# Three buffers for expert weights up to the last slots, and the last slot's weights requested before the second last's

## What is computed

```
gp = softmax(x @ w_rg + b_rg); gsel = top_k(gp, 1)          # 4 groups
ep = softmax(el_sel);          topv, topi = top_k(ep, 2)    # 2 of 4 experts in the group
weights = gp_sel * topv / sum(topv)
g = einsum('nd,edf->nef', x, w_e_gate)                      # w_e_gate, w_e_up: 16 x 1024 x 256
u = einsum('nd,edf->nef', x, w_e_up)
act = silu(g) * u * combine[:, :, None]
out = einsum('nef,efd->nd', act, w_e_down)                  # w_e_down: 16 x 256 x 1024
x = x + gate2 * out;  y = rms_norm(x, norm_final_g)
```

## Time and profile before

| what | us |
|---|---|
| median of 3 runs | 733.85 |
| lowest and highest of them | 733.02, 736.99 |
| the profiled execution, its own time | 732.28 |
| its span, first to last instruction | 730.4 |
| TensorE busy in it | 695.0 (95%) |
| VectorE, ScalarE, GpSimd busy | 538.0, 346.3, 212.1 |
| mean granted clock of TensorE | 0.986 |

### The profile page before, as it was taken

The page is one execution under the profiler, slowest core; times in us unless marked ns, Lnnn a source line. Parts: engine busy times, 40 slices in busy tenths (PEclk is TensorE's granted clock), DMA queues, the critical chain, the costliest instruction groups (busy, mean ns, idle before and its releaser), DMA issues.

```text
span 730.4 us, 11140 instructions
## 1 busy us (share of the span) xinstructions
PE 695.0 (95%) x4420; PEld 606.8 (83%) x4420; DVE 538.0 (74%) x782; ACT 346.3 (47%) x455; POOL 212.1 (29%) x89
## 2 busy tenths in 40 slices
PE   5899999999999999999999999998879999998995
PEld 2599989999898899999999998886368888887863
DVE  3547999999678865946556663656789999987887
ACT  4552232533243443447365121134378888777634
POOL 3004222222200000000000000000129999899486
PEclk9999999999999999999999999999799999999999
DMA  9964154556616336612325326165948999989865
GB/s 324 377 187 132 58 174 174 175 182 211 229 29 128 33 107 123 118 61 67 107 65 170 111 73 220 68 259 197 420 152 334 392 409 401 421 328 376 336 236 203
DMA packets 75607, 149.10 MB, mean 204 GB/s; under 512 B 11302, under 2 KB 54626, under 8 KB 68836
## 3 DMA queue, kind: packets, MB, share of 16 engines
q1 hardware_dynamic: 61572, 125.28, 49.8%
q10 hardware_dynamic: 10096, 12.63, 4.8%
q0 software_dynamic: 3888, 10.49, 4.2%
HBM read 138.29 MB, written 20.05 MB: 217 GB/s over the span
## 4 chain that ended last, share of the span: by engine, by line
PE 79%; DMA 8%; DVE 6%; issue 3%; ACT 3%; POOL 1%; ACTq 1%; DVEq 0%; POOLq 0%; SPq 0%
PE psum L1009 36%; PE psum L1285 8%; PE psum L1327 7%; PE psum L944 4%; PE psum L514 4%; PE psum L515 4%; PE psum L520 4%; DMA down_raw<-in_w_e_down 2%; DMA xg<-h_d,slot_b 2%; PE psum L1231 2%; DMA w_raw<-in_w_ada 2%; PE psum L1161 1%; PE psum L1463 1%; DMA w_raw<-in_w_e_up 1%; PE psum L1028 1%
## 5 line engine op out<-in xcount | busy, mean ns | idle before, releaser
L1009 PE MATMUL psum<-hh,w_h 128*128 128x320 f32 x608 | 144.7, 319 | 0.2 <-issue 0.2
L1009 PE MATMUL psum<-hh,w_l 128*128 128x320 f32 x608 | 138.5, 309 | 0.0
L1009 PE MATMUL psum<-hl,w_h 128*128 128x320 f32 x608 | 138.4, 309 | 0.0
L1009 PEld LDWEIGHTS psum<-hh,w_h 128*128 128x128 f32 x608 | 99.8, 188 | 6.1 <-issue 4.0
L2070 DVE SCALAR_TENSOR_TENSOR psum<-conv,taps,psum 128x760 f32<-128x760 f32 x100 | 101.5, 1015 | 3.4
L1009 PEld LDWEIGHTS psum<-hl,w_h 128*128 128x128 f32 x608 | 101.6, 188 | 0.0
L1009 PEld LDWEIGHTS psum<-hh,w_l 128*128 128x128 f32 x608 | 101.6, 188 | 0.0
L692 POOL TENSOR_TENSOR ob<-obh,toff 128x260 bf16<-128x260 f32 x1 | 2.0, 1993 | 331.7 <-DVE obh L600 331.7
L726 POOL TENSOR_TENSOR down_l<-down_raw,down_h 128x2048 fp32r<-128x2048 f32 x16 | 87.6, 5477 | 21.2 <-ACT down_h L1838 20.9
L936 POOL TENSOR_TENSOR w_l<-w_raw,w_h 128x2048 fp32r<-128x2048 f32 x9 | 42.1, 4682 | 141.3 <-ACT w_h L1519 141.3
L2356 DVE TENSOR_TENSOR w_l<-w_raw,w_h 128x2048 fp32r<-128x2048 f32 x26 | 74.5, 2868 | 11.4 <-ACT w_h L1844 11.4
(11 more groups left out here) (384 smaller groups left out, 1395.8 us busy)
## 6 DMA issues: line engine op xcount, KB each, us to landing
w_raw<-in_w_in SPq DMA_DIRECT2D x20, 1024.0 KB, 7.0
down_raw<-in_w_e_down SPq DMA_DIRECT2D x17, 1024.0 KB, 12.5
w_raw<-in_w_ada SPq DMA_DIRECT2D x16, 1024.0 KB, 9.5
w_raw<-in_w_e_gate SPq DMA_DIRECT2D x13, 1024.0 KB, 7.2
w_raw<-in_w_e_up SPq DMA_DIRECT2D x13, 1024.0 KB, 11.0
w_more<-in_w_ada SPq DMA_DIRECT2D x8, 1024.0 KB, 10.1
y_d<-yy ACTq DMA_DIRECT2D x15, 512.0 KB, 8.1
y_d<-in_x_sample SPq DMA_DIRECT2D x12, 512.0 KB, 8.1
```

The source lines that it names most:

```text
L1009: mm = pe.matmul(psum[:, p + q, 0:HALF], w, r[:, k, q * HALF:(q + 1) * HALF], start=(k == 0 and x == 0), stop=(k == KT - 1 and x == 2))
```

## The change

Three buffers stay in use to the end: also inside the loops slot numbers map to buffers 1 and 2, and the very last slot gets buffer 0 (`final`), last used by slot 12. The down weights get a mapping of their own, `down_buffer`. All engines' loops now begin at slot 13 (`LOOP_AT`), GpSimd's gathers known up to slot 14. The waits inside SP's loop come from a table `wait_i` that `late_tables` fills with four more VectorE operations. At the end SP requests the last slot's gate and up weights before the second last's. The selection matrix `onehot0` moves, since its place now is in use by slot 15, and GpSimd waits for slot 15's down matmuls before the last two of `rows_back`. Early on, down weights 2 and 0 change places in the queue.

```
-POOL_LOOP_AT = 11
-SP_LOOP_AT = 15
-THREE_UNTIL = POOL_LOOP_AT
-FEWER = 2
...
+        held = r1[:, 19, 0:NS]
+        for n in range(2):
+            then(dve.tensor_scalar(held, iota[:, 0:NS], float(LOOP_AT + 2 - n), -2.0, ALU.is_ge, ADD))
+            then(dve.tensor_tensor(wait_i[:, n, :], held, iota[:, 0:NS], ADD))
...
-    def buffer(b, s):
-        return (0, 2, 1)[b % 3] if isinstance(b, int) and b < THREE_UNTIL else s
+    def buffer(b, s, final=False):
+        return (0, 2, 1)[b % 3] if isinstance(b, int) else 0 if final else 1 + s
+
+    def down_buffer(b, s, final=False):
+        return (1, 2, 0)[b % 3] if isinstance(b, int) else 0 if final else 1 + s
...
-        for b in range(POOL_LOOP_AT):
+        for b in range(LOOP_AT - 1):
             known_gather(b + 3)
             low(b % 2, b)
         pairs = pair_count(pool)
-        with pool.Fori(POOL_LOOP_AT // 2, pairs - 2) as p:
-            for b, s, _ in pair_slots(p):
-                counted_gather(1 - s, b + 3)
-                low(s, b)
-        counted_gather(0, 2 * pairs)
-        low(1, 2 * pairs - 3)
+        with pool.Fori(LOOP_AT // 2, pairs - 1) as p:
+            counted_gather(1, 2 * p + 3)
+            low(0, 2 * p)
+            counted_gather(0, 2 * p + 4)
+            low(1, 2 * p + 1)
...
         for t in range(NT):
+            if t == NT - 1:
+                pool.wait_ge(e_used, 2 * pairs)
+                carry(1, row_i[:, 0, 0:1])
             rows_back(t, 0, ysum[:, t, :])
...
-        down_weights(0, 0, own(0))
-        sp.wait_ge(h2_st, 16 * (NT + 1))
         down_weights(2, 0, own(2))
-        gate_up(3, 1, own(3))
-        for b in range(4, SP_LOOP_AT):
-            gate_up(b, b % 2, own(b))
-            down_weights(b - 1, 1 - b % 2, own(b - 1))
+        sp.wait_ge(h2_st, 16 * (NT + 1))
+        down_weights(0, 0, own(0))
+        gate_up(3, 1, own(3), 1)
+        for b in range(4, LOOP_AT):
+            gate_up(b, b % 2, own(b), b - 2)
+            down_weights(b - 1, 1 - b % 2, own(b - 1), b - 3)
         pairs = pair_count(sp)
-        with sp.Fori(SP_LOOP_AT // 2, pairs) as p:
+        with sp.Fori(LOOP_AT // 2, pairs - 1) as p:
             for b, s, _ in pair_slots(p):
-                gate_up(b, s, by_table(b))
-                down_weights(b - 1, 1 - s, by_table(b - 1))
-        down_weights(2 * pairs, 0, by_table(2 * pairs))
+                held = reuse(0, b), reuse(1, b - 1)
+                gate_up(b, s, by_table(b), held[0])
+                down_weights(b - 1, 1 - s, by_table(b - 1), held[1])
+        gate_up(2 * pairs, 0, by_table(2 * pairs), LOOP_AT, final=True)
+        down_weights(2 * pairs - 2, 0, by_table(2 * pairs - 2), 2 * pairs - 3)
+        gate_up(2 * pairs - 1, 1, by_table(2 * pairs - 1), 2 * pairs - 2)
+        down_weights(2 * pairs - 1, 1, by_table(2 * pairs - 1), 2 * pairs - 2)
+        down_weights(2 * pairs, 0, by_table(2 * pairs), final=True)
```

More of the change, by code:

```diff
@@ L724, in low @@
             pool.wait_ge(d_hi, b + 1)
-            n = buffer(b, s)
+            n = down_buffer(b, s)
             pool.tensor_tensor(down_l[n][:, :], down_raw[n][:, :], down_h[:, s, :].bitcast(F32), SUB).then_inc(d_lo, 1)
@@ L821, in _, with gate_up @@
                                  modrow[v:P:GRP, :]).then_inc(mod_st, 16)
-        def gate_up(b, s, pick):
-            n = buffer(b, s)
+        def gate_up(b, s, pick, used=None, final=False):
+            n = buffer(b, s, final)
+            if used is not None:
+                sp.wait_ge(gu_done, used)
             for c, name in enumerate(("w_e_gate", "w_e_up")):
@@ L830, in gate_up, with down_weights, reuse @@
                         chunk_used(sp, G0 - RING + 2 * n + c)
-                else:
-                    sp.wait_ge(gu_done, b - 2 if isinstance(b, int) and b <= THREE_UNTIL + 1 else b - 1)
                 dst, landed = (third_raw[:, c, :], more_in[c]) if n == 2 else (w_raw[:, 2 * n + c, :], raw_in[2 * n + c])
                 sp.dma_start(dst.rearrange("p (k n) -> p k n", k=KT), pick(a[name], "(p k) n -> p k n")).then_inc(landed, 16)
[L836 to L841, removed]
+        def down_weights(b, s, pick, used=None, final=False):
+            n = down_buffer(b, s, final)
+            if used is not None:
+                sp.wait_ge(e_used, used)
             sp.dma_start(down_raw[n][:, :].rearrange("p (k n) -> p k n", k=2),
                          pick(a["w_e_down"], "(p k) n -> p k n")).then_inc(down_in[n], 16)
+        def reuse(n, b):
+            return sp.value_load(wait_i[0:1, n, bass.ds(b, 1)], min_val=LOOP_AT - 3, max_val=NS)
         def own(b):
@@ L1402, in down @@
         def down(s, b, first=False, last=False):
-            wh, wl = down_h[:, s, :], down_l[buffer(b, s)][:, :]
+            wh, wl = down_h[:, s, :], down_l[down_buffer(b, s, last)][:, :]
             cols = lambda w, j, q: w[:, j * D + q * 512:j * D + (q + 1) * 512]
@@ L1425, in slot @@
                 turn_x(1 - s, u + s, b + 1)
-            wh, wl = w_h[:, 2 * s:2 * s + 2, :], low_of(b, s)
+            wh, wl = w_h[:, 2 * s:2 * s + 2, :], low_of(b, s, last)
             both = lambda w, k: w[:, :, k * DE:(k + 1) * DE]
@@ L1831, in _, with w_hi @@
                         act.dma_start(x2[:, t, :], src).then_inc(x2_in, 16)
-        def w_hi(s, b, u, c):
-            n = buffer(b, s)
-            landed = 16 * loads(b, s, u)
+        def w_hi(s, b, u, c, final=False):
+            n = (down_buffer if c == 2 else buffer)(b, s, final)
+            landed = 16 * (down_loads if c == 2 else loads)(b, s, u, final)
             if c == 2:
@@ L1843, in w_hi @@
                     act.wait_ge(raw_in[2 * n + c], landed + 16 * loads_of_slot(G0 + 2 * n + c) - 16)
[L1844 removed]
+                act.activation(w_h[:, 2 * s + c, :], raw_of(b, s, c, final), ACT.Copy).then_inc(e_hi, 1)
         for t in range(NT):
@@ L1914, in _, with slot @@
             x_high(0, 0, q, True)
-        def slot(b, s, u, last=False):
+        def slot(b, s, u, last=False, before_last=False):
             early = b if isinstance(b, int) else 2
@@ L1931, in slot @@
             act.activation(sil[:, :], psum[:, s, 0:DE], ACT.Silu).then_inc(sil_done, 1)
-            w_hi(s, b, u, 2)
+            w_hi(s, b, u, 2, last)
             if last:
@@ L1943, in _ @@
                 slot(*one)
-        slot(*pair_slots(pairs - 1)[0])
+        slot(*pair_slots(pairs - 1)[0], before_last=True)
         slot(*pair_slots(pairs - 1)[1], last=True)
```

31 lines of the change are left out of this document (17 added, 14 removed).

## The result

The changed kernel takes 739.43 us (median of 8 runs, 738.62 to 742.81); the kernel before, run beside it, 733.75. The ratio is 1.0089, 95% interval 1.0069 to 1.0109: slower, by 5.7 us in the medians and by 5 to 8 us by the interval. The profiled execution has its own time of 738.62, a span of 736.8 against 730.4 (+6.4), and a mean granted clock of 0.984 against 0.986.

The account below looks back on a forecast made before the run. It took the DMA engines to set the expert stage's pace by slot 9, 10.27 us a slot. 7.9 (late matmuls) + 1.6 (clock) - 0.2 (small parts) = +9.3 us, 743.2 us against the median; range 738.5 to 747.0.

Parts of the forecast that it names:

- rival B: DMA engines' mean share counts and ScalarE's later steps absorb part: slot 15 late by 2 to 5 us, 738; chance 0.10.
- The earlier requests for slots 13 and 14: Weights of slots 13 and 14 asked for one slot, 9.3 us, earlier; taken alone worth 0 to 1 us.
- The exchange of holes: TensorE's 2.12 us wait for slot 14's gather closes; 2.1 us come back waiting for slot 15's gather.
- The place in the queue: In SP's queue slot 15's gate/up weights pass behind three transfers: down 13, gate/up 16 and down 14.
- Landing of slot 15's up weights: Up to 685.2 us, less recovered DMA idle time of 0 to 3.2, taken as 1.5: 683.7.
- a sign of being wrong: Slot 15's up weights landing by 677, or weights over 0.5 us a slot faster than 10.3 from slot 11 on.
- Landing to matmuls: From slot 15's up weights landing to its matmuls 4.4 us: start at 688.1 instead of 680.19, 7.9 us later.
- The clock: After TensorE's idling before slot 15, eight matmuls at the lower clock cost 1.6 us, bounds 0 and 3.2.
- Small parts: VectorE table operations, register loads, GpSimd's wait hidden; slot 15's early down weights save at most 0.2: counted -0.2 us.
- A: The request order at the end costs nothing, only the earlier requests count: -2.9 us, 731.0; chance 0.05.
- C: The change's two halves cancel, within 3 us of 733.85, the expert stage's DMA never pausing; chance 0.06.
- D: SP's waits hold gate/up 16 until gate/up 15 is due: 733 to 734; no chance of its own, within 0.06.

Follow-up runs that it names:

- old-order version: The changed kernel with slot 15's gate and up weights again requested before slot 16's, three buffers kept; 731.67 us, ratio 0.9969 to the kernel before.
- one transfer less: The changed kernel with slot 14's down weights requested after slot 15's gate and up weights, not before them; 736.03 us, ratio 1.0043.
- one MiB more: The changed kernel with an extra 1 MiB HBM-to-HBM copy in SP's queue behind slot 7's down weights; 742.20 us, ratio 1.0131.
- the version with the fillers in slot 15: The changed kernel with 27 filler matmuls on TensorE before slot 15, where it stood idle; 738.63 us, ratio 1.0080.
- the old order with known gathers: The changed kernel with slot 15's weights requested before slot 16's and slot 15's gather a known one too; 733.26 us, ratio 0.9979.

## Why the prediction was right, and where it was off

The sign and the mechanism held: slot 15's weights late behind three transfers, a hole of TensorE, the clock's fall behind it. The size did not: 739.4 is 3.8 us under the forecast of 743.2, and 0.5 under the 739.9 that the forecast's own bounds gave. It lies in the stated range of 738.5 to 747.0 because that was drawn into rival B, which is luck as much as judgement, for B's condition (slot 15 late by 2 to 5 us) was not met: it was late by 7.3. By its own steps, on the profiled executions (+9.3 forecast, +6.4 measured):

- The earlier requests for slots 13 and 14: 0 to 1 us forecast. The old-order version carries them, and its ratio of 0.9969 is 2.3 us (0.4 to 4.1). The forecast was at the low end of that. The exchange of holes came as told: slot 14's 2.12 us are gone, slot 15's gather makes one of 0.92, less than the 2.1 forecast. But an execution of the kernel before has 0.23 and 0.90 in these places, so the change is not shown to have brought the exchange.
- The place in the queue: shown, by the old order (the loss is gone), one transfer less (less lost) and one MiB more (more lost).
- Landing of slot 15's up weights: 683.7 forecast, 682.5 measured. This is a mis-sized term. The idle time of the DMA engines, 3.2 us by the mean share, was taken to be recovered by 1.5, because the last engine of each transfer had seemed busy right through. The landing came 2.7 us before the 685.2 of nothing recovered, 2.5 counted from slot 12's gate issue. Part shows between the down weights of slots 12 and 13: 658.35 and 667.30, 8.95 us apart, against 10.26 in the same place before. From slot 11 to 13 they come 9.4 us apart, over 0.5 us faster than 10.3, which the prediction had named as a sign of being wrong. Windows over the whole stretch, from slot 12's gate issue to the landing that ends the three transfers, before and after:

```profile
626.77:685.16 58.39, 55.98 (x274) 46.76 (x273) 48.05 (x43) 44.50 (x47) 48.19 (x20) 1.00 0.95 373
626.62:682.51 55.89, 50.16 (x242) 41.26 (x240) 39.75 (x36) 36.48 (x39) 41.30 (x16) 1.00 0.97 391
```

The bytes are the same (21.8 and 21.9 MB). The engines' mean idle time went from 3.1 to 2.0 us (the shares of the queues add up to 94.6% and 96.5% of the stretch), which is 1.2 of the 2.5; the hole of 640 to 646 was filled, but the one that follows is longer than before (share 0.69 in 664 to 670, 1.9 us). The other 1.3 us are a higher rate at the same share: 419 GB/s in 646 to 664 at 1.01, where the kernel before had 391 in 646 to 666 at 1.00. So the 1.5 us taken for idle time were about right, and what the sum lacked is that full engines moved more in a microsecond; why they did is open. The landing came nearly as early as with everything recovered (682.0, the premise of rival B), but only half by that reason.
- Landing to matmuls: 4.4 us forecast, 4.95 measured (682.5 to 687.45), of which 1.0 us are the ten transposes at the lower clock (2.41 us instead of 1.40), so 3.95 without the clock. Slot 15's matmuls are 7.26 us later than before, 6.25 without the clock; forecast 7.9.
- The clock: 1.6 us forecast in slot 15, 1.8 measured: 1.0 in the transposes, 0.8 in the next four matmuls, at 0.43, 0.43, 0.43 and 0.40 instead of 0.23. Sized well, and yet wrong in the sum: the fall of before at the start of the final sums, the very row from which the price was taken, is not there after. The final sums start 7.9 us late (707.35 against 699.47) and the kernel ends 6.4 late, and the first eight matmuls there, once 3.4 us, now take 1.9. This is the step that was missing: it added a fall without asking whether the old one would stay. That one fall took the other's place is likely by the version with the fillers in slot 15, and not shown, as said there.
- Small parts: -0.2 forecast; from slot 16's last gate/up matmul (+8.16) to the final sums (+7.9) it is -0.26. GpSimd's new wait costs nothing, as its timeline shows: `tick` has no idle time before it and the gather leaves 0.15 us after.

```profile
715.22 0.21 POOL L708 TENSOR_TENSOR tick<-row_i 128x1 int32<-128x1 int32 x1
715.58 1.04 POOL L757 DMA_INDIRECT ysum<-y_d,row_i  x1 [0.15 <-issue]
```

Together: 6.25 + 1.8 + 0.1 (the rest of slot 15) - 0.26 - 1.5 = 6.4. Against the forecast's 7.9 + 1.6 - 0.2 that is 1.65 less at the landing and the steps behind it, 0.3 more in slot 15, mostly its clock, and 1.5 less at the end, which the forecast did not have.

Of the rivals, A (the order is harmless) asked for a DMA 9 us further ahead; the up load took 13.42 us. C (the halves cancel) fell with the time, D (the change does not do what it says) with the issues at 636.11 and 654.78. The ceiling of 435 GB/s that the Trainium skill gives ("DMA: Bandwidth & Descriptors", Specifications) put the landing at 681.8, nearer to the 682.5 measured than the forecast was. That is luck: the 7.2 us were for the three loads alone, while the trace has a store and a gather beside them (1 MiB together at most, which at that ceiling, by the same estimate, is 2.4 us more), and the rate with the share full stayed under it (416 GB/s in 640 to 646, 425 in 626.6 to 640). That gathers keep their turn beside a full queue (the same page, "Queues, rings and completion order") the trace bears out once more: slot 15's gather, issued at 658.22 with slot 16's loads still in SP's queue, is there for TensorE at 669.48, 11.3 us later.

Open: why the clock falls in the final sums of some profiles and not of others with the same holes; what brings the higher rate of the full DMA engines; where the clock falls in the slower group of runs with one transfer less ahead; and whether known gathers cost the old-order version anything.

## What to carry to other kernels

Where a stage is bound by an in-order queue of transfers, a free buffer is no reason to ask early for what is needed last: the request takes its place from one needed sooner, and 1 MiB ahead moved the landing by 1.75 and 2.6 us in the two places tried, one of them over 60 us early. Idle time of the DMA engines, read as a mean share below 1, can in part be taken once more is queued, even if the landings look evenly spaced: here 1.2 of some 3 us, with as much again from a higher rate. And when a forecast adds a fall of the clock for a new stall, it must ask whether the falls that are already there will stay.

## What was not expected of the hardware

The granted clock fell in one place of a program and not in a like one. After 1.68 us idle in the 3.5 before 699.5 it was 0.51 for 3.5 us in the kernel before; after 1.82 us idle in the 5.3 before 707.3 it was 1.00 in the changed kernel, and after 1.88 us in the 5.5 before 697.5 it was 1.00 in the old-order version; in the old order with known gathers, after 1.87 us in the 6.2 before 700.2, it fell to 0.52 again. The windows of the old-order version:

```profile
692.00:697.50 5.50, 3.62 (x18) 2.91 (x16) 3.88 (x8) 3.55 (x5) 4.43 (x6) 1.00 0.41 117
697.50:701.00 3.50, 3.50 (x16) 2.89 (x17) 3.48 (x3) 0.00 (x0) 2.89 (x3) 1.00 0.92 321
```

And weights came faster in the changed kernel: 9.89 and 8.95 us for a slot's 3 MiB from slot 11 to 13, where six slots on end had taken 10.27 on the mean, with the DMA engines moving 419 GB/s at a full share where they had moved 391 to 402.
